# Six row groups per chunk on VectorE: three ahead of the last gate product instead of four, and two loads of u columns asked for earlier

## The chip, the cores and the metric

The kernel runs on one core of a Trainium2 chip. The metric is the device time of one execution in microseconds (us); lower is better. The engines of the core are named as the profile names them: PE (TensorE, matrix products), DVE (VectorE), ACT (ScalarE), POOL (GpSimd) and SP (SyncE, which here only starts transfers). Each has its own instruction stream, and they wait for each other by semaphores.

## The reference

One layer of a decoder trunk: window attention, RWKV-7 time mixing, a merge and a LayerNorm, and then the PEER layer, of which this case is about the last part. For every token, each of 8 heads picks 16 of 16384 single-neuron experts:

```
q = (xb @ peer_q).reshape(PEER_BLOCK, PEER_HEADS, 2, PEER_HALF)
s = jnp.einsum("bhcd,hckd->bhck", q, peer_keys)
sv, si = lax.top_k(s, PEER_TOPK)
...
gate = jax.nn.softmax(fv, axis=-1)
act = jax.nn.gelu(jnp.einsum("bhkd,bd->bhk", peer_u[eidx], xb))
return jnp.einsum("bhk,bhkd->bd", (gate * act), peer_v[eidx])
y = layer_norm(DEEPNORM_ALPHA * h + peer(h, ...), ln2_g, ln2_b)
```

The model width is 1024, all in float32. There are 1024 prompt tokens, which is 8 blocks of 128, and 8 sampled tokens.

## The kernel before, in words

The blocks' experts are computed in two ways. For the three **dense** blocks (`DENSE`) the kernel multiplies the 384 tokens with all 16384 rows of peer_u, applies Gelu, multiplies by a gate matrix G that is zero for experts that were not picked, and multiplies with all of peer_v. For the other blocks the rows of peer_u and peer_v that were picked are **fetched** one index column at a time by POOL (an indirect DMA brings 128 rows of 1024 floats, 0.52 MB), and DVE forms the dots and the weighted sums. The last three fetched blocks (`FETCHED_2`) run beside the dense blocks in the function `experts`, which is the last stage of the kernel.

`experts` walks over 16 chunks (`NCH`) of 8 tiles (`CH`) of 128 experts. In one chunk:

- PE's score stage: for each tile e, 8 matmuls over the width, from u columns (`u`) and the tokens (`hT`) into one of two PSUM buffers `sps`. The u columns lie in two pairs of tiles in SBUF, so `load_u(m)` may start when the score products of pair m-2 are done (`s_psum`). A pair is 1.05 MB.
- ACT applies Gelu to each tile of scores and writes it into `w`; DVE multiplies it by its part of G (`weigh`, the gate product).
- PE's v stage: for each of the three dense blocks k and each tile e, two matmuls of `w` with `v` into `vps`. For tile e it waits for the gate product of e (`w_done`). The v rows of a chunk (4.2 MB) are asked for when the v stage before is done, the gate matrix of a chunk (1.57 MB) when the last gate product before it is done.

All loads of u, v and G stand in SP's stream, in an order written out by hand. The row groups of the fetched blocks are woven in by hand too. One **group** on DVE (`rows.dve(dve, 8)`) is four dots, a small product of weights, four additions of rows from three groups before, and, for the first two of the three blocks, one part of the choice of experts for the next block. The fetched rows go through a ring of 10 buffers: POOL starts a fetch when DVE has used the buffer. There are 6 groups in a chunk (`PERC`), 96 in all, and three more rounds that only add. `before(e)` says how many groups stand in the slot of tile e, `behind(k)` how many stand behind the last gate product of the chunk. DVE's slot e is the gate product of tile e-2 and then the slot's group.

So in one chunk before the change DVE does: a group (slot 1), gate products 0 and 1, a group (slot 3), products 2 and 3, a group (slot 5), products 4 and 5, a group (slot 7), products 6 and 7, and two groups behind.

After the loop DVE does the last rounds of additions, the LayerNorm of the last fetched block, and those of the three dense blocks (lines 2890 to 2892).

## Time and profile before

| | us |
|---|---|
| median of 3 runs | 4342.94 (4333.28 to 4346.08) |
| the profiled execution, its time | 4383.67 |
| its span in the profile | 4381.5 |
| `experts`, from the first score product to the end of the span | 2948.75 to 4381.5 |
| PE busy in the whole span | 3782.8 (86%) |
| DVE busy in the whole span | 3027.9 (69%) |

The profiled execution takes 2.17 us more than its span, and 40.7 us more than the median of the runs. Chunks are counted from 0 to 15 here. PE's score stage of a chunk and its v stage each take about 41.4 us when nothing is waited for, 82.7 us together.

### The profile page before, as it was taken

The page shows a single profiled execution, that of the slowest core. Times are in us where ns is not written, and L with a number is a line of the kernel's source. Part 1 is how long each engine was busy: PE and PEld are TensorE (multiplying, and loading weights), DVE is VectorE, ACT ScalarE, POOL GpSimd, SP SyncE. Part 2 cuts the span into 40 slices and gives each one's busy share as a digit, 9 for nine tenths or more (in the row PEclk, how much of TensorE's full clock was granted, in tenths as well). Part 3 has the DMA queues.
Part 4 walks back from the last instruction along what each step waited for, and adds up shares of the span by engine and source line. Part 5 has one row for each costly group of instructions (what it writes and reads, how often), then busy time and mean ns, then how long its engine had stood idle before and what let it go on. Part 6 is the DMA issues. An engine that isn't in the chain of part 4 may idle for free. (4 is left out here: it accounts for less than half of the span.)

```text
span 4381.5 us, 71344 instructions
## 1 busy us (share of the span) xinstructions
PE 3782.8 (86%) x28107; PEld 2520.7 (58%) x28107; DVE 3027.9 (69%) x5964; ACT 974.3 (22%) x2046; POOL 1821.2 (42%) x1489
## 2 busy tenths in 40 slices
PE   6896888879989997888888786668999999999998
PEld 5775765546655556877765464564544454455444
DVE  0364422768988774777757378877889788977777
ACT  1351211104533332222221013770000000000001
POOL 0016100254432212333326107735666566666664
PEclk8997988889989998989989887679999999999999
DMA  7453453597766655666659633459999999999998
GB/s 191 121 163 109 154 172 146 200 359 245 264 239 235 243 206 208 225 229 227 219 209 381 247 129 50 95 155 396 403 406 391 399 412 412 382 410 413 413 403 316
DMA packets 400418, 1158.75 MB, mean 264 GB/s; under 512 B 78471, under 2 KB 157388, under 8 KB 382508
## 3 DMA queue, kind: packets, MB, share of 16 engines
q0 software_dynamic: 207216, 687.87, 43.5%
q1 hardware_dynamic: 151556, 422.07, 26.0%
q10 hardware_dynamic: 41311, 44.24, 3.0%
q8 instruction: 223, 3.65, 0.3%
q14 instruction: 112, 0.91, 0.1%
HBM read 1047.82 MB, written 116.80 MB: 266 GB/s over the span
## 5 line engine op out<-in xcount | busy, mean ns | idle before, releaser
L2814 PE MATMUL x_sps<-c_big,l_c_wo 128*128 128x384 f32 x2048 | 678.1, 493 | 33.9 <-DMA l_c_wo<-u_cols 30.2
L2822 PE MATMUL x_vps<-l_c_v,x_w 128*128 128x512 f32 x1536 | 676.9, 602 | 31.2 <-DVE x_w L2871 31.1
L387 POOL DMA_INDIRECT l_w_ring<-u_rows,k_eidx x256 | 299.6, 1170 | 922.2 <-DVE l_w_dots L443 424.3
L387 POOL DMA_INDIRECT w_ring<-u_rows,k_eidx x384 | 482.3, 1256 | 423.6 <-DVE w_dots L443 246.6
L2814 PEld LDWEIGHTS x_sps<-c_big,l_c_wo 128*128 128x128 f32 x2048 | 393.6, 193 | 318.9 <-DMA l_c_wo<-u_cols 37.4
L460 DVE SCALAR_TENSOR_TENSOR l_c_share<-w_ring,w_wts,l_c_share 128x1024 f32<-128x1024 f32 x384 | 493.4, 1285 | 76.0 <-DMA w_ring<-v_rows,k_eidx 63.0
L2822 PEld LDWEIGHTS x_vps<-l_c_v,x_w 128*128 128x128 f32 x1536 | 296.0, 193 | 406.1 <-issue 363.5
L387 POOL DMA_INDIRECT w_ring<-v_rows,k_eidx x384 | 413.1, 1076 | 143.9 <-issue 112.0
L387 POOL DMA_INDIRECT l_w_ring<-v_rows,k_eidx x256 | 300.7, 1175 | 327.0 <-DVE l_w_yacc L460 261.8
L683 PE MATMUL l_pzp<-c_big,l_c_w 128*128 128x384 f32 x960 | 327.5, 499 | 46.6 <-DMA l_c_w<-w_tiles 46.6
L460 DVE SCALAR_TENSOR_TENSOR l_w_yacc<-l_w_ring,l_w_wts,l_w_yacc 128x1024 f32<-128x1024 f32 x256 | 328.9, 1285 | 24.9 <-DMA l_w_ring<-v_rows,k_eidx 16.3
L443 DVE CUSTOM_DVE_ANT_0 w_ring<-w_ring,w_h 128x1024 f32<-128x1024 f32 x256 | 301.2, 1222 | 30.5 <-DMA w_ring<-u_rows,k_eidx 15.8
L443 DVE CUSTOM_DVE_ANT_0 l_w_ring<-l_w_ring,l_w_h 128x1024 f32<-128x1024 f32 x256 | 305.3, 1223 | 17.8 <-DMA l_w_ring<-u_rows,k_eidx 11.3
L2846 ACT ACTIVATE x_w<-x_sps 128x384 f32<-128x384 f32 x128 | 62.9, 491 | 1069.1 <-PE x_sps L2814 1001.6
L683 PEld LDWEIGHTS l_pzp<-c_big,l_c_w 128*128 128x128 f32 x960 | 185.2, 196 | 174.2 <-DMA l_c_w<-w_tiles 47.5
L1015 PE MATMUL l_qzp<-c_big,l_c_w 128*128 128x385 f32 x768 | 266.3, 502 | 14.8 <-ACT l_qz L1119 8.0
L2413 POOL DMA_INDIRECT s_G<-l_f_at_gate,l_f_at_u x128 | 208.1, 1626 | 122.3 <-DVEq L2597 68.7
L1015 PEld LDWEIGHTS l_qzp<-c_big,l_c_w 128*128 128x128 f32 x768 | 149.1, 197 | 125.0 <-issue 34.0
L2363 PE MATMUL l_f_gps<-l_f_two,l_f_one 128*128 128x128 f32 x512 | 102.8, 364 | 73.7 <-ACT l_f_two L2471 63.3
L2871 DVE TENSOR_TENSOR x_w<-x_w,l_c_wo 128x384 f32<-128x384 f32 x128 | 67.9, 559 | 132.7 <-ACT x_w L2846 123.9
L443 DVE CUSTOM_DVE_ANT_0 w_ring<-w_ring,l_c_share 128x1024 f32<-128x1024 f32 x128 | 149.6, 1220 | 5.7 <-DMA w_ring<-u_rows,k_eidx 5.2
L683 PE MATMUL e_pzp<-c_big,e_c_w 128*128 128x264 f32 x480 | 117.7, 405 | 31.9 <-DMA e_c_w<-w_tiles 20.6
(672 smaller groups left out, 6198.9 us busy)
## 6 DMA issues: line engine op xcount, KB each, us to landing
l_c_wo<-u_cols SPq DMA_DIRECT2D x64, 1024.0 KB
l_c_v<-v_rows SPq DMA_DIRECT2D x32, 2048.0 KB
e_c_w<-w_tiles SPq DMA_DIRECT2D x54, 512.0 KB, 3.6
l_c_w<-w_tiles SPq DMA_DIRECT2D x54, 512.0 KB
l_c_wo<-s_G SPq DMA_DIRECT2D x16, 1536.0 KB
s_rw<-l_q_out SPq DMA_DIRECT2D x48, 384.0 KB
s_G<-l_c_share ACTq DMA_DIRECT2D x8, 2048.0 KB
s_zT<-l_pz ACTq DMA_DIRECT2D x30, 384.0 KB
```

The source lines that it names most:

```text
L387: pool.indirect_dma_start(out=self.ring[:, r, :], out_offset=None, in_=self.A[table], in_offset=bass.IndirectOffsetOnAxis(ap=idx[:, s:s + ...
L443: V.tensor_tensor_reduce(ring[:, q % self.RING, :], ring[:, q % self.RING, :], self.h[b % self.HB][:, :], 1.0, 0.0, ALU.mult, ALU.add, sel ...
L460: self.mark(dve, V.scalar_tensor_tensor(ya[:, :], self.ring[:, q % self.RING, :], self.wts[:, s:s + 1], ya[:, :], ALU.mult, ALU.add), self ...
L683: mm = pe.matmul(zp[v % 2][:, 0:GN], w[u % 3][:, k, :], xT[:, k, x0 + g * GN:x0 + (g + 1) * GN], start=(k == 0), stop=(k == KT - 1))
L1015: mm = pe.matmul(zp[s][:, g, 0:GZ], w[q][:, k, :], xT[:, k, g * GZ:(g + 1) * GZ], start=(k == 0), stop=(k == KT - 1))
L2363: mm = pe.matmul(gps[q % 2][:, t * NKEY:(t + 1) * NKEY], one[q % 2][:, t, :], two[q % 2][:, t, :], start=True, stop=True)
L2413: pool.indirect_dma_start(out=matrix, out_offset=bass.IndirectOffsetOnAxis(ap=at_u[:, s:s + 1], axis=0), in_=gates[:, s:s + 1], in_offset= ...
L2814: mm = pe.matmul(sps[n % 2][:, 0:ND * P], u[n % 4][:, k, :], hT[:, k, :], start=(k == 0), stop=(k == KT - 1))
L2822: mm = pe.matmul(vps[k][:, x * 512:(x + 1) * 512], w[:, e, k * P:(k + 1) * P], v[:, e, x * 512:(x + 1) * 512], start=(c == 0 and e == 0), ...
L2846: act.activation(w[:, e, :], sps[n % 2][:, 0:ND * P], ACT.Gelu).then_inc(S["act_done"], 1)
L2871: V.tensor_tensor(w[:, e, :].rearrange("p (g t) -> p g t", t=TGW), w[:, e, :].rearrange("p (g t) -> p g t", t=TGW), G[:, :, e, :], ALU.mul ...
```

## The change

The number of tiles whose slots may hold a group goes from 4 to 3: the group of slot 7 is taken out from between the gate products 5 and 6, and stands behind product 7, where there are now three groups instead of two. The second edit is in SP's stream ahead of the loop: the third pair of u columns is asked for ahead of the wait for the gate matrix's stores, and the fourth right behind the load of the gate matrix, ahead of what `rows.begin` starts (the scores of the block to be chosen, the next block's h and the LayerNorm weights). Before, both pairs stood in slots 1 and 3 of chunk 0, behind all of these.

```
-        before = lambda e: 1 if e % 2 and e // 2 < PERC else 0
-        behind = lambda k: len(range(CH // 2 + k, PERC, ND))
+        AMID = CH // 2 - 1
+        before = lambda e: 1 if e % 2 and e // 2 < min(PERC, AMID) else 0
+        behind = lambda k: len(range(AMID + k, PERC, ND))
...
             rows.load_h(sp, 0)
+            load_u(2)
             for j in range(2):
                 sp.wait_ge(g_out[j], G_STORES)
             load_g(0)
+            load_u(3)
             rows.begin(sp, 1)
             for c in range(NCH):
                 for e in range(CH):
-                    if e in (1, 3):
+                    if c and e in (1, 3):
                         load_u((CH * c + e + 3) // 2)
                     rows.sp(sp, before(e))
```

SP's stream at the start of `experts` before the change. `w_h<-s_h` is the first fetched block's h, `l_c_wo<-s_G` the gate matrix, `k_scs<-s_sc` the scores for the choice, `l_c_share` the next h and the LayerNorm weights, `l_c_wo<-u_cols` a pair of u columns.

```order
L330 DMA w_h<-s_h 128x1024
L2763 DMA l_c_wo<-s_G 128x3072
L335 DMA k_scs<-s_sc 128x2048
L330 DMA l_c_share<-s_h 128x1024
L350 DMA l_c_share<-ln 128x2048
L2753 DMA l_c_wo<-u_cols 128x2048 x4
L2763 DMA l_c_wo<-s_G 128x3072
```

The same place with the change:

```order
L330 DMA w_h<-s_h 128x1024
L2754 DMA l_c_wo<-u_cols 128x2048
L2764 DMA l_c_wo<-s_G 128x3072
L2754 DMA l_c_wo<-u_cols 128x2048
L335 DMA k_scs<-s_sc 128x2048
L330 DMA l_c_share<-s_h 128x1024
L350 DMA l_c_share<-ln 128x2048
L2754 DMA l_c_wo<-u_cols 128x2048 x2
L2764 DMA l_c_wo<-s_G 128x3072
```

One pair has moved ahead of the gate matrix, one between the gate matrix and the scores; two of the four stay where they were.

DVE's stream in the last chunk before the change, from the end of the group of slot 5 to the end of the group of slot 7 and the products behind it (`x_w<-x_w,l_c_wo` is a gate product, a dot is a row with `w_ring,w_dots`, an addition one with `l_c_share<-w_ring`):

```order
L460 SCALAR_TENSOR_TENSOR l_c_share<-w_ring,w_wts,l_c_share 128x1024 x4
L2871 TENSOR_TENSOR x_w<-x_w,l_c_wo 128x384 x2
L443 ISA w_ring,w_dots<-w_ring,w_h 128x1024
L443 ISA w_dots 128x1
...
L450 TENSOR_TENSOR w_wts<-w_dots,k_gate 128x4
L460 SCALAR_TENSOR_TENSOR l_c_share<-w_ring,w_wts,l_c_share 128x1024 x4
L2871 TENSOR_TENSOR x_w<-x_w,l_c_wo 128x384 x2
```

The same place with the change:

```order
L460 SCALAR_TENSOR_TENSOR l_c_share<-w_ring,w_wts,l_c_share 128x1024 x4
L2874 TENSOR_TENSOR x_w<-x_w,l_c_wo 128x384 x4
L443 ISA w_ring,w_dots<-w_ring,w_h 128x1024
L443 ISA w_dots 128x1
...
L450 TENSOR_TENSOR w_wts<-w_dots,k_gate 128x4
L460 SCALAR_TENSOR_TENSOR l_c_share<-w_ring,w_wts,l_c_share 128x1024 x4
```

The four gate products 4 to 7 now stand together, and the group that parted them comes behind them. The streams of PE, ACT and POOL are unchanged, but for ACT's place for that group's Gelu, which is between the same instructions.

## Rows read from the trace of the kernel before

**Rows 1.** Stretches: engines' busy us, TensorE's granted clock, DMA share, GB/s.

```profile
2948.70:3049.00 100.30, 87.63 (x224) 44.94 (x225) 70.03 (x143) 6.10 (x15) 62.28 (x54) 0.91 0.99 387
3049.00:3841.20 792.20, 757.43 (x2017) 386.44 (x2016) 684.80 (x1213) 47.88 (x132) 502.36 (x430) 0.98 1.01 401
3841.20:4278.20 437.00, 422.18 (x1122) 215.87 (x1121) 324.50 (x441) 28.88 (x76) 281.10 (x243) 0.98 1.02 411
...
3980.00:4066.00 86.00, 82.19 (x219) 41.90 (x218) 62.82 (x85) 4.71 (x14) 55.44 (x48) 0.98 1.02 413
```

**Rows 2.** Waits in `experts`, by engine: total us, times, longest us.

```profile
DVE x_w L2871 <- ACT x_w L2846: 123.9, 29, 11.1
...
PE x_vps L2822 <- DVE x_w L2871: 31.1, 7, 7.9
PE x_sps L2814 <- DMA l_c_wo<-u_cols: 30.2, 9, 12.6
```

**Rows 3.** PE in order of time, chunk 8: start, us, [idle before it <-releaser].

```profile
3698.91 10.46 PE L2822 MATMUL x_vps<-l_c_v,x_w 128*128 128x512 f32 x24
3715.53 33.64 PE L2822 MATMUL x_vps<-l_c_v,x_w 128*128 128x512 f32 x72 [6.15 <-DVE x_w L2871]
```

**Rows 4.** DVE in order of time, chunk 8: the gate products around slot 7.

```profile
3701.05 1.03 DVE L2871 TENSOR_TENSOR x_w<-x_w,l_c_wo 128x384 f32<-128x384 f32 x2
...
3714.92 1.02 DVE L2871 TENSOR_TENSOR x_w<-x_w,l_c_wo 128x384 f32<-128x384 f32 x2
```

**Rows 5.** PE in order of time, chunk 0 and the score stage of chunk 1.

```profile
2948.75 22.76 PE L2814 MATMUL x_sps<-c_big,l_c_wo 128*128 128x384 f32 x64 [2.88 <-PEq L146]
2984.13 23.85 PE L2814 MATMUL x_sps<-c_big,l_c_wo 128*128 128x384 f32 x64 [12.62 <-DMA l_c_wo<-u_cols]
3007.81 41.36 PE L2822 MATMUL x_vps<-l_c_v,x_w 128*128 128x512 f32 x96
3049.01 41.44 PE L2814 MATMUL x_sps<-c_big,l_c_wo 128*128 128x384 f32 x128
```

**Rows 6.** SP's queue, chunks 0 and 1: start and us of issuing.

```profile
2961.53 0.43 SPq L335 DMA_DIRECT2D k_scs<-s_sc  x1
...
2962.95 45.39 SPq L2753 DMA_DIRECT2D l_c_wo<-u_cols  x4
...
3049.21 0.81 SPq L2758 DMA_DIRECT2D l_c_v<-v_rows  x2
3059.53 0.33 SPq L2753 DMA_DIRECT2D l_c_wo<-u_cols  x1
```

**Rows 7.** DVE, chunk 0: the first step of the choice.

```profile
2974.01 0.29 DVE L168 MAX8 k_sv<-k_scs 128x8 f32<-128x128 f32 x1 [8.13 <-DMA k_scs<-s_sc]
```

**Rows 8.** Stretches, as rows 1, in which the DMA engines moved less.

```profile
3000.00:3010.00 10.00, 10.00 (x31) 5.55 (x30) 9.75 (x15) 1.17 (x4) 7.75 (x6) 1.00 0.80 269
...
3290.00:3320.00 30.00, 30.00 (x79) 14.82 (x78) 29.23 (x39) 0.56 (x2) 17.92 (x17) 1.00 0.91 335
3730.00:3750.00 20.00, 20.00 (x49) 8.95 (x48) 19.37 (x41) 0.00 (x0) 14.91 (x12) 1.00 0.93 331
3810.00:3840.00 30.00, 30.00 (x68) 13.05 (x67) 28.36 (x39) 0.20 (x1) 23.80 (x20) 0.95 0.95 345
```

**Rows 9.** DVE at the end: last gate products, first dots of the next groups.

```profile
4325.52 1.03 DVE L2871 TENSOR_TENSOR x_w<-x_w,l_c_wo 128x384 f32<-128x384 f32 x2
4326.47 1.22 DVE L443 CUSTOM_DVE_ANT_0 w_ring<-w_ring,w_h 128x1024 f32<-128x1024 f32 x1
...
4336.52 1.22 DVE L443 CUSTOM_DVE_ANT_0 w_ring<-w_ring,w_h 128x1024 f32<-128x1024 f32 x1
```

**Rows 10.** PE, from the score stage of chunk 13 on, and chunk 15.

```profile
4122.15 23.16 PE L2814 MATMUL x_sps<-c_big,l_c_wo 128*128 128x384 f32 x64 [4.76 <-DMA l_c_wo<-u_cols]
...
4278.16 20.80 PE L2814 MATMUL x_sps<-c_big,l_c_wo 128*128 128x384 f32 x64
...
4303.95 20.80 PE L2814 MATMUL x_sps<-c_big,l_c_wo 128*128 128x384 f32 x64
```

More of the change, by code:

```diff
@@ L2743, in experts @@
         B = len(FETCHED_2)
-        before = lambda e: 1 if e % 2 and e // 2 < PERC else 0
-        behind = lambda k: len(range(CH // 2 + k, PERC, ND))
+        AMID = CH // 2 - 1
+        before = lambda e: 1 if e % 2 and e // 2 < min(PERC, AMID) else 0
+        behind = lambda k: len(range(AMID + k, PERC, ND))
         assert sum(before(e) for e in range(CH)) + sum(behind(k) for k in range(ND)) == PERC
@@ L2765, in _ @@
             rows.load_h(sp, 0)
+            load_u(2)
             for j in range(2):
@@ L2768, in _ @@
             load_g(0)
+            load_u(3)
             rows.begin(sp, 1)
@@ L2771, in _ @@
                 for e in range(CH):
-                    if e in (1, 3):
+                    if c and e in (1, 3):
                         load_u((CH * c + e + 3) // 2)
```

## The prediction, made before the changed kernel was run

> **What bounds the kernel now.** The change touches only the last stage, from 2948.75 to the end of the span at 4381.5 [rows 5], so I read that stage alone, first by stretches, then by waits, then PE and DVE in order of time. The stretches show three engines close to full at once: over chunks 1 to 14 PE is busy 1179.6 of 1229.2 us, DVE 1009.3, and the DMA share stands at 1.01 and 1.02, with 401 and 411 GB/s [rows 1]. The best stretch moved 413 GB/s, which I take as full speed [rows 1]. So the reader should see a kernel in which PE is the longest chain by a little, and in which transfers leave hardly any room: chunks 1 to 14 moved 401 x 792.2 + 411 x 437.0 = 497.3 MB, which at 413 GB/s takes 1204 us. They took 1229. The transfers' room is 25 us, and in chunk 0 another 6 us (387 x 100.3 = 38.8 MB, 94 us at full speed).
>
> The waits say what PE loses: 31.1 us in 7 waits for a gate product and 30.2 us in 9 for u columns, 12.6 of them in chunk 0 [rows 2]. One of the seven, chunk 8, shows the mechanism: PE does tiles 0 to 5 of the v stage (24 rows of 96, three quarters of the first block's third) and idles 6.15 us, until 3715.53 [rows 3]. DVE meanwhile did products 4 and 5 at 3701.05, then a group of 12.9 us, and only then products 6 and 7, at 3714.92 [rows 4]. Their scores were ready when PE's score stage ended, at 3699 [rows 3]. The group stands between.
>
> **The change part by part.**
>
> *The group of slot 7 behind the gate products.* In chunk 8 products 6 and 7 would follow at 3702, 9 us before the v stage asks for tile 6 at 3709.4, and the wait is gone. No wait of the seven is longer than 7.9 us [rows 2], less than the group that goes. What is late next: four groups now stand in a row (three behind, and slot 1 of the next chunk), and then product 0. Scores of tile e are ready about 5.2 x (e+1) us after the score stage begins (41.44 us for 8 tiles [rows 5]). Four groups of 12.9 us are 51.6, from the end of one score stage over a v stage of 41.3; product 0 comes some 11 us into the next score stage instead of 6. Tiles 0 to 3 have room, but tile 4 now stands behind only two more groups: 11 + 26 + 2 = 39 us, and PE asks for it at 41.4 + 6.9 = 48.3. So there are 9 us of room where three groups ahead of tile 6 left none (11 + 39 + 2 against 51.7). Where the choice has its heaviest parts two groups fill the 30 us from 3290 (DVE busy 29.23 of them [rows 8]), 15 us each; then it is 60 - 41 + 30 + 2 = 51, a wait of some 3 us. I keep two such waits, 6 of the 31.1 us: 25 us of PE's waits go.
>
> *The two pairs of u columns.* PE ended its first four tiles at 2971.5 and waited 12.62 us for the third pair, asked for at 2962.95 behind the gate matrix, the scores, an h and the weights [rows 5, 6]. Now it is asked for once two tiles are scored, at about 2960, and only rows are in flight: 1.05 MB beside them, there long before 2971.5. The second half then ran 23.85 us where half of a later stage is 20.7 [rows 5]; the granted clock of the stage is 0.91 [rows 1], so part of it ran at 1.2 GHz after the idle time, and those 3.1 us go too: 15.7 us. The fourth pair is asked for when four tiles are scored, at 2971.5, and is needed at 2982. The price is that this wait now stands ahead of the scores for the choice: asked for at 2961.53 and there at 2974.0 [rows 6, 7], they go out at 2972 and land behind one pair, at about 2980. DVE begins products 0 and 1 some 6 us late, but it then has one group fewer ahead of the last product. It ends its fourth group near 3012, as before, and PE starts the v stage at about 2992.5 instead of 3007.8. I cost the delay at nothing; without this cover it is 6 us.
>
> *The end.* Here the change costs. In the last chunk the score stage ends at 4324.8, products 6 and 7 come at once, at 4325.52, and from there DVE's groups follow each other without a gap [rows 9, 10]. A group without choice takes 4336.52 - 4326.47 = 10.05 us [rows 9]. With the change, products 6 and 7 still can't come ahead of the scores; DVE idles while it could have done the group, and does it behind. The end of the kernel is 10.05 us further from PE's last score stage. Nothing hides it, since these additions and three LayerNorms follow in DVE's own stream.
>
> *The sum.* PE's last score stage could begin 25 + 15.7 = 40 us earlier, if the transfers can follow. The trace of before can't show that, so I bound it. Upper end: 40 us. It exceeds the transfers' room of 31, but DVE idled 11.1 us for the last chunk's product 0 [rows 2], and with a group fewer ahead of product 7 may come another 10 us late without moving the end, so about 20 us of fetches can be put off into the last chunk. Lower end: only the stretches that ran slow behind a wait that goes are won. In the v stages that a gate wait lengthened, DVE alone draws on the transfers, more slowly than they can deliver: 30 us at 335 GB/s, 20 at 331, 30 at 345, and 10 at 269 in chunk 0 [rows 8]. Against 413 these are 5.7 + 4.0 + 4.9 + 3.5 = 18 us. I take the middle, 29 us, because both ends rest on stretches of this stage and neither is nearer. 29 - 10 = 19 us off the profiled execution's 4383.67, to 4365. The runs' median is 40.7 us below that execution; I take the same 19 us off it: 4324 us.
>
> **A rule that speaks against it.** A v load is asked for at 3049.21 and a pair of u columns behind it at 3059.53, and PE used that pair at 3069.7 with no wait [rows 5, 6]. So SP's queue brought 5.24 MB in 20.5 us, 256 GB/s or 62% of the whole, beside a row ring that had work throughout. The Trainium skill (DMA: Bandwidth & Descriptors, Queues, rings and completion order) says that each DMA engine goes round the queues that have work, a packet from each, and takes a queue's descriptors in order. If that meant halves, the 5.24 MB would take 25.4 us at 206 GB/s, and PE would wait 4.7 us in every chunk. The trace disagrees for most chunks, so the sum leaves it out.
>
> **The rivals.**
>
> *The transfers swallow it.* PE runs ahead and meets u columns and starved groups instead; the last score stage begins 0 to 18 us earlier, and the end lies between 8 us earlier and 10 later: 4335 to 4353, middle 4343. For it speaks a DMA share of 1.01, against it that the slow stretches lie just behind the waits that go. That the change does not do what it says (its waits come back at other tiles) ends here as well. Chance 0.25.
>
> *Slower by u waits.* With PE ahead the ring never fills, SP's queue gets a smaller share in the score stages, and u columns come late as in chunk 13: 4.76 us and 23.16 - 20.7 = 2.4 us at the lower clock [rows 10], 7.2 us a chunk. From six more such chunks on, 43 us, the kernel is slower by over 13 us; in all 14, 101 - 40 + 10 = 71 us slower, 4414. The 62% above speak against it. Chance 0.07.
>
> *Slower by DVE.* If DVE never idles, a chunk takes 6 groups and 4.5 us of gate products. Its busy time less 63 us of products is 946 us for 84 groups, 11.3 each, 12.2 with its waits for rows: 78 us, well under PE's 82.7. Against the present 87.8 us a chunk it decides from a group of 13.9 us on; at 14.2 it would be 6 x 0.3 x 14 = 25 us slower at the last score stage, 4378 with the end. Chance 0.05.
>
> **How the numbers follow.** A measurement of this kernel tells a change from none at about 0.3%, which is 13 us: under 4330 is faster, above 4356 slower. The forecast has chance 0.63 and its own range 4313 to 4335; some 0.11 of it lies above 4330. Faster 0.52, same 0.11 + 0.25 = 0.36, slower 0.12. The range reaches from 4304, a little beyond the case in which all of PE's 40 us come through, to 4350, which takes in nearly all of the first rival.
>
> **What would show it.** PE waits for gate products under 10 us in total, and none in chunks 8 and 9 over 3. No wait for the third pair, a v stage of chunk 0 from about 2993, DVE's first choice step near 2980. The last score stage at about 4249 instead of 4278. DVE idle before the last chunk's product 7, and from there to its last instruction 10 us more than before. Slow stretches in the v stages of chunks 3, 8 and 9 gone. I am wrong if u waits beyond chunk 0 grow past 35 us, or if the last score stage begins after 4260.

## The result, and the profile after

The changed kernel takes 4354.60 us (median of 15 runs, 4341.94 to 4366.03) beside 4344.34 (15 runs of the kernel before on the same chip, 4330.77 to 4361.09). The ratio is 1.0028, with a 95% interval of 1.0017 to 1.0039: about 12 us slower, within the 0.3% that the prediction called no change, and on the other side of it than the forecast.

The profiled execution of the changed kernel took 4342.70 us (span 4340.5), 41 us less than that of the kernel before. This is no contradiction: `experts` began at 2906.22 instead of 2948.75, so 42.5 us of the difference lie in stages that the change does not touch, and come from one execution to the next. From here on I compare lengths inside `experts`, not times since the start, and use several profiles of each kernel.

Here are the stretches of the changed kernel, with columns as in [rows 1]: chunk 0, chunks 1 to 14, the last chunk to the end of the span, and then three of its slow stretches.

```profile
2906.20:2993.60 87.40, 84.98 (x224) 43.67 (x225) 55.18 (x113) 6.33 (x15) 49.64 (x43) 0.97 0.99 381
2993.60:4226.60 1233.00, 1177.06 (x3138) 600.84 (x3137) 1018.62 (x1679) 78.20 (x208) 772.18 (x677) 0.98 1.01 404
4226.60:4340.50 113.90, 87.75 (x237) 44.61 (x235) 87.79 (x110) 14.63 (x35) 53.90 (x50) 0.90 0.83 316
...
3250.00:3260.00 10.00, 10.00 (x27) 4.94 (x26) 9.82 (x14) 0.00 (x0) 6.78 (x6) 1.00 0.71 228
...
3690.00:3700.00 10.00, 10.00 (x27) 4.78 (x26) 9.69 (x19) 0.00 (x0) 5.72 (x6) 1.00 0.91 320
...
3750.00:3790.00 40.00, 35.85 (x80) 15.95 (x81) 39.09 (x55) 0.41 (x2) 25.71 (x22) 0.91 0.91 324
```

For the kernel before, [rows 1] cuts chunks 1 to 14 differently and leaves out the last chunk, so this is the same view of it in the same cuts:

```profile
3049.00:4278.20 1229.20, 1179.62 (x3138) 602.30 (x3137) 1009.29 (x1654) 76.76 (x208) 783.46 (x673) 0.98 1.01 404
4278.20:4381.50 103.30, 87.75 (x237) 44.61 (x235) 81.77 (x103) 14.74 (x35) 49.64 (x42) 0.94 0.81 310
```

Three things stand in these rows. Chunk 0 is 13 us shorter (87.40 instead of 100.30). The last chunk is 10.6 us longer (113.90 instead of 103.30). And the fourteen chunks between, where 25 us of waits were to go, take 1233.0 instead of 1229.2 us, at the same 404 GB/s. Multiplied out, the bytes say the same: before, 38.8 + 496.6 + 32.0 = 567.4 MB in the three parts; after, 33.3 + 498.1 + 36.0 = 567.4 MB. The shorter chunk 0 moved 5.5 MB less, which then had to be moved later: 1.5 MB of it in chunks 1 to 14, 4.0 MB in the last chunk.

The 404 GB/s are a mean of two parts. Here are chunks 1 to 10 and chunks 11 to 14, first of the kernel before, then of the changed one:

```profile
3049.00:3924.20 875.20, 840.21 (x2242) 428.93 (x2241) 749.04 (x1302) 55.36 (x149) 555.66 (x477) 0.98 1.01 402
3924.20:4278.20 354.00, 339.41 (x898) 173.38 (x897) 260.25 (x353) 21.40 (x59) 227.80 (x196) 0.97 1.02 410
```

```profile
2993.60:3874.20 880.60, 841.15 (x2241) 428.98 (x2240) 751.61 (x1319) 56.45 (x149) 554.86 (x481) 0.98 1.01 401
3874.20:4226.60 352.40, 335.91 (x898) 171.87 (x897) 267.01 (x361) 21.74 (x59) 217.32 (x197) 0.98 1.02 413
```

The last four of them run at 413 GB/s with the change, for 352 us; the first ten stay at 401. The slow stretches above lie among these ten, in the v stages of chunks 3, 8 and 9, and those are the three chunks in which [rows 8] has them before. In all of them DVE is busy nearly throughout (9.82 of 10 us, 9.69 of 10, 39.09 of 40). So 413 can be held with all loads, and what the changed kernel did not do is hold it in chunks 1 to 10.

The waits of the changed kernel inside `experts`, with columns as in [rows 2] and DVE's waits for fetched rows added:

```profile
DVE l_c_share L460 <- DMA w_ring<-v_rows,k_eidx: 141.7, 76, 4.9
DVE w_ring L443 <- DMA w_ring<-u_rows,k_eidx: 60.9, 28, 9.6
PE x_vps L2825 <- DVE x_w L2874: 44.4, 10, 8.8
DVE x_w L2874 <- ACT x_w L2849: 14.3, 5, 4.5
PE x_sps L2817 <- DMA l_c_wo<-u_cols: 14.0, 10, 7.4
```

PE's gate waits did not go from 31.1 to 6 us, they went to 44.4 in 10 waits. What did go are DVE's waits for scores, 123.9 us before and 14.3 now. In their place DVE waits 203 us for fetched rows; before it was 84 (63.0 and 21.0). DVE has hardly any slack in front of PE any more, and what it waits for is rows.

Chunk 9 shows how this looks. First PE, as in [rows 3], then DVE, as in [rows 4]:

```profile
3697.06 41.44 PE L2817 MATMUL x_sps<-c_big,l_c_wo 128*128 128x384 f32 x128
3738.34 7.03 PE L2825 MATMUL x_vps<-l_c_v,x_w 128*128 128x512 f32 x16
3754.15 36.08 PE L2825 MATMUL x_vps<-l_c_v,x_w 128*128 128x512 f32 x80 [8.78 <-DVE x_w L2874]
```

```profile
3708.47 1.28 DVE L460 SCALAR_TENSOR_TENSOR l_c_share<-w_ring,w_wts,l_c_share 128x1024 f32<-128x1024 f32 x1 [0.80 <-DMA w_ring<-v_rows,k_eidx]
...
3713.42 1.28 DVE L460 SCALAR_TENSOR_TENSOR l_c_share<-w_ring,w_wts,l_c_share 128x1024 f32<-128x1024 f32 x1 [3.67 <-DMA w_ring<-v_rows,k_eidx]
3716.01 1.28 DVE L460 SCALAR_TENSOR_TENSOR l_c_share<-w_ring,w_wts,l_c_share 128x1024 f32<-128x1024 f32 x1 [1.30 <-DMA w_ring<-v_rows,k_eidx]
...
3722.24 1.03 DVE L2874 TENSOR_TENSOR x_w<-x_w,l_c_wo 128x384 f32<-128x384 f32 x2
...
3753.54 1.96 DVE L2874 TENSOR_TENSOR x_w<-x_w,l_c_wo 128x384 f32<-128x384 f32 x4
```

Product 0 comes 25 us into the score stage (3722.24 less 3697.06), not 11. The four additions of the group ahead of it wait for their rows one by one. Products 4 to 7 follow two groups later, at 3753.54, and PE, which had finished 16 of 96 rows of its v stage, idles 8.78 us. All ten gate waits of the changed kernel stand there, ahead of the last 80 matmuls of a v stage: the wait is now for tile 4. In the 10 us from 3690, just ahead of this score stage, transfers ran at 320 GB/s, and 20 us later DVE waited for them.

In chunk 0 the second edit did what it said. PE's start of the stage, as in [rows 5]:

```profile
2906.22 43.72 PE L2817 MATMUL x_sps<-c_big,l_c_wo 128*128 128x384 f32 x128 [2.88 <-PEq L146]
2949.78 7.03 PE L2825 MATMUL x_vps<-l_c_v,x_w 128*128 128x512 f32 x16
2959.21 34.60 PE L2825 MATMUL x_vps<-l_c_v,x_w 128*128 128x512 f32 x80 [2.40 <-DVE x_w L2874]
```

PE's 128 score matmuls run without a break, and the v stage begins 43.6 us into the stage instead of 59.1. The first choice step on DVE, as in [rows 7], stood 25.3 us into the stage and now stands 35.6 us into it:

```profile
2941.84 0.29 DVE L168 MAX8 k_sv<-k_scs 128x8 f32<-128x128 f32 x1 [21.13 <-DMA k_scs<-s_sc]
```

At the end, as in [rows 9], the last gate product and the first dot behind it:

```profile
4268.63 1.49 DVE L2874 TENSOR_TENSOR x_w<-x_w,l_c_wo 128x384 f32<-128x384 f32 x3
4273.71 0.56 DVE L2874 TENSOR_TENSOR x_w<-x_w,l_c_wo 128x384 f32<-128x384 f32 x1 [3.59 <-ACT x_w L2849]
4274.19 1.22 DVE L443 CUSTOM_DVE_ANT_0 w_ring<-w_ring,w_h 128x1024 f32<-128x1024 f32 x1
...
4284.24 1.22 DVE L443 CUSTOM_DVE_ANT_0 w_ring<-w_ring,w_h 128x1024 f32<-128x1024 f32 x1
```

DVE idles for the last score and then has one group of 10.05 us more to do than before; it is busy 87.79 us in this part instead of 81.77.

### The profile page after: what moved, and what is told of

Its sections match the earlier page's. It is cut to its first block and busy times, and to the rows that moved or that the text cites. A ratio compares the mean times of both kernels' runs of the same rounds, so it can differ in the third digit from the quotient of the medians.

```text
span 4340.5 us, 71344 instructions
## 1 busy us (share of the span) xinstructions
PE 3751.0 (86%) x28107; PEld 2506.1 (58%) x28107; DVE 3029.2 (70%) x5964; ACT 975.3 (22%) x2046; POOL 1794.3 (41%) x1489
## 3 DMA queue, kind: packets, MB, share of 16 engines
q0 software_dynamic: 207216, 687.87, 43.9%
## 5 line engine op out<-in xcount | busy, mean ns | idle before, releaser
L2825 PE MATMUL x_vps<-l_c_v,x_w 128*128 128x512 f32 x1536 | 679.3, 603 | 44.4 <-DVE x_w L2874 44.4
L387 POOL DMA_INDIRECT w_ring<-u_rows,k_eidx x384 | 462.6, 1205 | 409.1 <-DVE w_dots L443 201.1
L2817 PEld LDWEIGHTS x_sps<-c_big,l_c_wo 128*128 128x128 f32 x2048 | 390.3, 191 | 297.6 <-DMA l_c_wo<-u_cols 20.9
L683 PE MATMUL l_pzp<-c_big,l_c_w 128*128 128x384 f32 x960 | 325.0, 496 | 47.2 <-DMA l_c_w<-w_tiles 47.2
L2413 POOL DMA_INDIRECT s_G<-l_f_at_gate,l_f_at_u x128 | 205.9, 1608 | 123.1 <-DVEq L2597 68.0
L2363 PE MATMUL l_f_gps<-l_f_two,l_f_one 128*128 128x128 f32 x512 | 103.5, 365 | 73.0 <-ACT l_f_two L2471 66.5
L2363 PEld LDWEIGHTS l_f_gps<-l_f_two,l_f_one 128*128 128x128 f32 x512 | 89.3, 262 | 85.7 <-ACT l_f_two L2471 73.2
```

The source lines that it names most:

```text
L387: pool.indirect_dma_start(out=self.ring[:, r, :], out_offset=None, in_=self.A[table], in_offset=bass.IndirectOffsetOnAxis(ap=idx[:, s:s + ...
L683: mm = pe.matmul(zp[v % 2][:, 0:GN], w[u % 3][:, k, :], xT[:, k, x0 + g * GN:x0 + (g + 1) * GN], start=(k == 0), stop=(k == KT - 1))
L2363: mm = pe.matmul(gps[q % 2][:, t * NKEY:(t + 1) * NKEY], one[q % 2][:, t, :], two[q % 2][:, t, :], start=True, stop=True)
L2413: pool.indirect_dma_start(out=matrix, out_offset=bass.IndirectOffsetOnAxis(ap=at_u[:, s:s + 1], axis=0), in_=gates[:, s:s + 1], in_offset= ...
L2817: mm = pe.matmul(sps[n % 2][:, 0:ND * P], u[n % 4][:, k, :], hT[:, k, :], start=(k == 0), stop=(k == KT - 1))
L2825: mm = pe.matmul(vps[k][:, x * 512:(x + 1) * 512], w[:, e, k * P:(k + 1) * P], v[:, e, x * 512:(x + 1) * 512], start=(c == 0 and e == 0), ...
```

## The experiments

**Theory 1**, the first rival of the prediction: transfers bind chunks 1 to 14, and what PE gains at one tile it loses at another. **Theory 2**: the late scores of the block to be chosen put DVE behind from chunk 0 on, and it never recovers. **Theory 3**: DVE's own work, not its rows, binds it. Two later theories, **A** and **B**, are given where they come up.

All runs together, in us. "Stage" is `experts` from the first score product to the end of the span of one profiled execution; chunk 0, 1 to 14 and the last are its parts; "gate" is PE's waits at the tile boundaries of the v stages, where it waits for a gate product (the profile names no releaser for some of them and calls them "issue": 11.2 us in e7_before_again, 2.7 in e8_after_again, 10.8 in e12_split_v, 1.6 in e5_before_no_v, 21.2 in e11_before_copy_v; they are counted); the ratio is that of run times to the kernel before on the same chip, with its interval.

| run | stage | chunk 0 | 1 to 14 | last | gate | ratio |
|---|---|---|---|---|---|---|
| before | 1432.8 | 100.3 | 1229.1 | 103.3 | 31.1 | |
| e7_before_again | 1429.6 | 97.3 | 1229.0 | 103.4 | 26.3 | |
| after | 1434.3 | 87.4 | 1232.9 | 113.9 | 44.4 | 1.0028 (1.0017 to 1.0039) |
| e8_after_again | 1452.6 | 86.9 | 1252.9 | 112.7 | 37.4 | |
| e15_after_third | 1437.4 | 87.6 | 1236.9 | 112.9 | 47.2 | |
| e1_rows | 1442.6 | 97.0 | 1232.9 | 112.7 | 43.9 | 1.0029 (1.0016 to 1.0041) |
| e2_u | 1432.4 | 100.0 | 1228.9 | 103.5 | 49.6 | 1.0016 (1.0003 to 1.0030) |
| e3_u_scores | 1426.2 | 94.3 | 1225.8 | 106.1 | 39.2 | 0.9995 (0.9980 to 1.0010) |
| e4_last | 1435.7 | 86.8 | 1235.9 | 113.0 | 49.1 | 1.0006 (0.9992 to 1.0019) |
| e14_last_again | 1429.0 | 87.7 | 1226.2 | 115.1 | 35.4 | |
| e12_split_v | 1429.2 | 94.4 | 1231.4 | 103.5 | 43.5 | 0.9980 (0.9967 to 0.9993) |
| e5_before_no_v | 1370.1 | 97.0 | 1169.7 | 103.4 | 10.0 | 0.9861 (0.9816 to 0.9907) |
| e6_after_no_v | 1358.4 | 86.6 | 1159.0 | 112.7 | 2.3 | 0.9858 (0.9794 to 0.9922) |
| e13_last_no_v | 1345.3 | 87.2 | 1154.7 | 103.4 | 2.6 | 0.9841 (0.9780 to 0.9902) |
| e9_copy_at_s | 1488.3 | 87.4 | 1288.1 | 112.7 | 58.9 | 1.0141 (1.0114 to 1.0168) |
| e10_copy_at_v | 1496.8 | 87.5 | 1286.2 | 123.1 | 69.6 | 1.0129 (1.0099 to 1.0158) |
| e11_before_copy_v | 1495.7 | 97.1 | 1288.2 | 110.4 | 96.3 | 1.0131 (1.0101 to 1.0161) |

### The same kernels again

Runs e7_before_again, e8_after_again and e15_after_third have no edit. They tell how far one profile can be trusted.

> The kernel before once more, for a second profile of it: how far experts' stage (1433 us) and its waits (31 us for gate products, 18 for u columns behind chunk 0) differ between two executions. Expected within 5 us for the stage, with up to 40 us of difference ahead of it.

> The changed kernel once more. Expected: experts' stage 1434 to 1446 us, last chunk 113 to 114, gate waits 35 to 50 us, most of them at tile 4. If the median's 10 us lie in the stage, it is nearer to 1443 than to 1434.

> The changed kernel for a third profile (stage 1434.3 and 1452.6 before). Expected: chunk 0 at 87 us, chunks 1 to 14 at 1233 to 1253, last chunk 112.7 to 114, so a stage 5 to 15 us above the 1431 of the kernel before.

The second profile of the kernel before has the same 1229.0 us in chunks 1 to 14. Its waits view names 15.1 us of gate waits, where the first had 31.1, but two more stand at the same place (behind 24 matmuls of a v stage) without a releaser. Here is the longer one, of chunk 3, on PE, and DVE's products 6 and 7 that end it:

```profile
3265.69 33.73 PE L2822 MATMUL x_vps<-l_c_v,x_w 128*128 128x512 f32 x72 [7.74 <-issue]
```

```profile
3265.08 1.02 DVE L2871 TENSOR_TENSOR x_w<-x_w,l_c_wo 128x384 f32<-128x384 f32 x2
```

With both (7.74 and 3.50 us, in chunks 3 and 6) the gate waits are 26.3 us in 6 waits beside 31.1 in 7: the waits that the change goes for do repeat. The 4.8 us fewer did not make the fourteen chunks shorter; waits for u columns in them are 24.2 us beside 17.6. The changed kernel took 1232.9, 1252.9 and 1236.9 us there, with gate waits of 44.4, 37.4 and 47.2. The 1252.9 is an outlier that I cannot place; its transfers ran at 399 GB/s, and PE idled 70 us in it, beside 56 in the first profile. Chunk 0 (86.9 to 87.6) and the last chunk (112.7 to 113.9) repeat well. The means over profiles, 2 and 3 of them, give chunk 0 -11.5, chunks 1 to 14 +11.9, the last +9.8: together 10 us slower, near the 12 that the runs show.

### One half of the change at a time

**e1_rows**: the kernel before with DVE's new order, and SP's stream as it was.

```diff
-        before = lambda e: 1 if e % 2 and e // 2 < PERC else 0
-        behind = lambda k: len(range(CH // 2 + k, PERC, ND))
+        AMID = CH // 2 - 1
+        before = lambda e: 1 if e % 2 and e // 2 < min(PERC, AMID) else 0
+        behind = lambda k: len(range(AMID + k, PERC, ND))
```

> Only the row groups are moved; SP's stream is that of before. Theory 1 (the transfers bound chunks 1 to 14, so what PE wins at product 6 is lost to starved groups, and the end costs 10 us): experts' stage 1440 to 1446 us against 1433 in the profile of before, ratio 1.002 to 1.003; the last chunk 113 to 114 us from its score stage to the end of the span. Theory 2 (the scores that come 10 us later behind the fourth pair leave DVE behind for good, and this is what brings the gate waits back): without that edit the gate waits fall under 20 us and the last score stage begins over 10 us earlier than before, ratio 0.998 to 1.000.

Gate waits of 43.9 us without the late scores (the first choice step came 22.1 us into the stage): Theory 2 falls. DVE's new order by itself keeps chunk 0 at 97.0, adds 3.8 us to chunks 1 to 14 and 9.3 to the last, 13 us against e7_before_again (10 against the first profile); the runs show 13 (ratio 1.0029). The changed kernel has the same ratio, 1.0028, although its chunk 0 is 10 us shorter (87.4 beside 97.0): what the second edit gains in chunk 0 is not seen in the whole.

**e2_u**: the changed kernel with DVE's old order, so only SP's stream differs from before.

```diff
-        AMID = CH // 2 - 1
+        AMID = CH // 2
```

> Only the two pairs of u columns are asked for earlier; DVE's order is that of before. Theory 1: chunk 0 is 12 to 15 us shorter, chunks 1 to 14 give nearly all of it back, last chunk 103 us as before: ratio 0.998 to 1.001. Theory 2: DVE starts 10 us late and stays behind, more gate waits than before (over 40 us): ratio 1.001 to 1.003.

Chunk 0 gained nothing, 100.0 us. PE has no wait for u columns there but two for gate products. PE in chunk 0:

```profile
2957.56 7.03 PE L2825 MATMUL x_vps<-l_c_v,x_w 128*128 128x512 f32 x16
2966.87 3.70 PE L2825 MATMUL x_vps<-l_c_v,x_w 128*128 128x512 f32 x8 [2.28 <-DVE x_w L2874]
2980.51 34.04 PE L2825 MATMUL x_vps<-l_c_v,x_w 128*128 128x512 f32 x72 [9.94 <-DVE x_w L2874]
```

With four groups ahead of product 7 there is no cover for scores that come 10 us later: DVE waits 20.6 us for them, its groups slip, and PE waits for tile 6 (24 rows done, as in [rows 3]) 9.94 us. The u wait of 12.6 us turned into this one. The numbers are those that were expected by Theory 2 (49.6 us of gate waits, ratio 1.0016), and chunk 0 is not the 12 to 15 us shorter of Theory 1. But DVE doesn't stay behind: 12.2 of the gate waits lie in chunk 0, product 0 comes 6 to 11 us into the score stage from chunk 1 on, as before, and chunks 1 to 14 take 1228.9 us. So the late scores cost time in chunk 0 alone.

**e3_u_scores**: e2_u, with the scores asked for ahead of the fourth pair.

```diff
             load_g(0)
-            load_u(3)
             rows.begin(sp, 1)
+            load_u(3)
```

> Only the u columns earlier, DVE's order as before, but what brings the scores for the choice stands ahead of the fourth pair. DVE's first choice step should come 26 to 28 us after the first score product instead of 36. Theory 1: the time is that of the run with both pairs ahead, within 0.1%. Theory 2: 0.2 to 0.3% faster than that run, ratio 0.996 to 0.998 to the kernel before.

DVE had the scores at 30.6 us into the stage, still later than the 26 to 28 that I expected:

```profile
2960.03 0.29 DVE L168 MAX8 k_sv<-k_scs 128x8 f32<-128x128 f32 x1 [16.10 <-DMA k_scs<-s_sc]
```

The 9.94 us wait is gone, a u wait of 7.62 stays, and chunk 0 takes 94.3. The profile has the shortest stage of all kernels with their full loads, 1426.2 us, but the runs cannot tell it from before. Against e2_u it is 6 us faster (medians 4345.77 and 4351.97 on the same chip), 0.14%, about the 5.7 us by which chunk 0 is shorter. That is more than the 0.1% of Theory 1 and less than the 0.2 to 0.3% of Theory 2.

**e4_last** and **e14_last_again** (the same kernel twice): the changed kernel, with the old order of DVE in the last chunk alone. `before` and `behind` take the chunk as an argument everywhere.

```diff
-        AMID = CH // 2 - 1
-        before = lambda e: 1 if e % 2 and e // 2 < min(PERC, AMID) else 0
-        behind = lambda k: len(range(AMID + k, PERC, ND))
+        AMID = lambda c: CH // 2 if c == NCH - 1 else CH // 2 - 1
+        before = lambda c, e: 1 if e % 2 and e // 2 < min(PERC, AMID(c)) else 0
+        behind = lambda c, k: len(range(AMID(c) + k, PERC, ND))
```

> The changed kernel, but with four groups ahead of the last gate product in chunk 15 alone. Both theories: the last chunk falls from 114 to 103 or 104 us, so 10 us (0.23%) less than the changed kernel. Theory 1: with that the kernel is level with before, ratio 0.998 to 1.001. If it stays at 1.002 or more, the cost is not at the end.

> The same order in chunk 15 with all loads, for a second profile: its first had a last chunk of 113.0 us, although its ratio was 1.0006. If DVE is late at the last score stage (groups of slots 3 and 5 begin over 2 us later than 11.5 and 22.5 into it), the last chunk stays near 113; if it is in time, 103 to 105.

The runs improve on those of the changed kernel (1.0006 beside 1.0028, intervals that just overlap), but the profiles don't show it where it was expected: the last chunk takes 113.0 and 115.1 us, not 103. (The profiled execution of e4_last is the slowest of its 12 runs, 4377.53 us where their median is 4351.83.) DVE in the last chunk of e14_last_again, whose score stage begins at 4238.18:

```profile
4251.69 1.28 DVE L460 SCALAR_TENSOR_TENSOR l_c_share<-w_ring,w_wts,l_c_share 128x1024 f32<-128x1024 f32 x1 [4.88 <-DMA w_ring<-v_rows,k_eidx]
...
4257.97 1.03 DVE L2873 TENSOR_TENSOR x_w<-x_w,l_c_wo 128x384 f32<-128x384 f32 x2
...
4294.29 1.03 DVE L2873 TENSOR_TENSOR x_w<-x_w,l_c_wo 128x384 f32<-128x384 f32 x2
```

The last two products come at 56.1 us into the stage (4294.29), where before they came at 47.4 [rows 9, 10]. The groups of slots 3 and 5 begin 20.9 and 34.8 us into it, not 11.5 and 22.5, so the case of a late DVE in the expectation is the one that came. DVE reached the last chunk waiting for rows, and in these two profiles the rows and not the place of the group decide when the last product can be done. Whether this holds for the other runs is not shown: their ratio of 1.0006 is what the order's 10 us would give.

### Fewer bytes, and the same bytes elsewhere

**e5_before_no_v** and **e6_after_no_v**: the kernels before and after without the v loads of chunks 1 to 15 (63 MB of 567), so that PE multiplies with chunk 0's rows of peer_v.

```diff
                     rows.sp(sp, behind(k))
-                if c + 1 < NCH:
-                    load_v(c + 1)
...
                         pe.wait_ge(S["w_done"], CH * c + e + 1)
-                        if c and e % QUAD == 0:
-                            pe.wait_ge(v_in[e // QUAD], 16 * c)
```

> The kernel before, but chunks 1 to 15 load no rows of peer_v and use those of chunk 0, so 4.2 of 35 MB a chunk are not moved; that part of the result is left out. Theory 1: with 12% fewer bytes the transfers no longer bind; u waits vanish and gate waits fall under 15 us, since groups are no longer starved in the score stage; chunks 1 to 14 take 83 to 84 us each. Theory 3 (DVE's own work binds, whatever the transfers): gate waits stay near 31 us, chunks near 86.

> The changed kernel with the same part left out. Theory 1: gate waits under 10 us, chunks 1 to 14 at 83 us each, so the last score stage begins as early as in the run before or up to 15 us earlier, and the end costs its 10 us: ratio of this run to the run before 0.999 to 1.002. Theory 3: gate waits stay over 30 us, at tile 4.

Chunks 1 to 14 of e5_before_no_v:

```profile
3043.90:4213.60 1169.70, 1159.10 (x3137) 596.56 (x3136) 1009.53 (x1654) 76.41 (x208) 767.98 (x672) 1.00 0.97 373
```

and of e6_after_no_v:

```profile
3023.00:4182.00 1159.00, 1155.29 (x3137) 595.71 (x3136) 1022.78 (x1685) 77.30 (x208) 777.26 (x678) 1.00 0.98 380
```

In e6_after_no_v PE is busy 1155.3 of 1159.0 us at the full granted clock, and its gate waits in the whole stage are 2.3 us. DVE did the same work as in the changed kernel, 1022.8 us of it, and was in time: Theory 3 falls. With 12% fewer bytes in a chunk the change does between these two kernels what the prediction said in kind: 10.4 us off chunk 0, 10.7 off chunks 1 to 14 with 10.0 us of gate waits to win, and 9.3 more in the last chunk. Of the 10.7, 9.7 are chunk 9 (92.2 to 82.5 us), where e5_before_no_v still waits 6.38 us for tile 6 at 353 GB/s: that wait is DVE's order and the choice in its groups, not transfers, and with all loads the change turns it into one of 8.78 us for tile 4. These are single profiles. The runs, with intervals of half a per cent, are too coarse to show the 12 us that this leaves.

**e13_last_no_v**: e6_after_no_v with e4_last's order of the last chunk.

> The changed kernel with four groups ahead of the last gate product in chunk 15 alone, and without the v loads of chunks 1 to 15 (their rows are replaced by those of chunk 0). With those bytes gone DVE is not late when the last score stage begins. If the end costs 10 us because the third group stands behind the last gate product, the last chunk falls from 112.7 (changed kernel without v loads) to 103 or 104 us here. If it stays over 110, the end of the changed kernel is longer for another reason.

Here the forecast's term for the end stands by itself. DVE at the end:

```profile
4207.01 1.03 DVE L2869 TENSOR_TENSOR x_w<-x_w,l_c_wo 128x384 f32<-128x384 f32 x2
4207.95 1.22 DVE L443 CUSTOM_DVE_ANT_0 w_ring<-w_ring,w_h 128x1024 f32<-128x1024 f32 x1
```

The last products come 47.4 us into the last chunk (its score stage began at 4159.64), exactly as in [rows 9, 10], and the chunk takes 103.4. The 9.3 us beside e6_after_no_v's 112.7 are the price of the group's place; nothing else differs between the two kernels.

**Theory A**: the bytes of a chunk bind, wherever in the chunk they are moved. **Theory B**: the v load at the start of a score stage starves the group of slot 1 there, and elsewhere in the chunk it would not. **e9_copy_at_s** moves the same v bytes as the changed kernel at the same place, but into device memory, so that PE doesn't wait for them. **e10_copy_at_v** moves them half a chunk earlier, beside the v stage ahead. **e11_before_copy_v** does this to the kernel before. In all three PE again multiplies with chunk 0's rows.

```diff
             def load_v(c):
-                sp.wait_ge(S["v_psum"], ND * c)
                 for a in range(CH // QUAD):
-                    sp.dma_start(v[:, QUAD * a:QUAD * (a + 1), :], A["v_quads"][CH // QUAD * c + a]).then_inc(v_in[a], 16)
+                    sp.wait_ge(v_in[a], 16 * (c - 1))
+                    sp.dma_start(A["spare"][a], A["v_quads"][CH // QUAD * c + a]).then_inc(v_in[a], 16)
...
                         load_u(CH // 2 * (c + 1) + m)
+                    load_v(c + 1)
                     load_g(c + 1)
...
-                if c + 1 < NCH:
-                    load_v(c + 1)
```

(In e9_copy_at_s the first wait and the place of the call stay as they were.)

> The changed kernel in which chunks 1 to 15 use the peer_v rows of chunk 0 (their own are left out of the result), but the same 4.2 MB are still read, at the same place (start of the score stage), into a spare array in device memory. It shows whether the copy stands for the load. Both theories: chunks 1 to 14 near 1230 us again (1159 without the bytes), gate waits over 30 us at tile 4, product 0 over 12 us into the score stage in most chunks.

> As the run with the copy at the score stage, but the 4.2 MB are asked for at the start of the v stage ahead, where the slow stretches lie. Theory A (the bytes of a chunk bind, wherever they stand): chunks 1 to 14 within 10 us of that run. Theory B (the v load at the start of the score stage starves just the group of slot 1 that the change leaves there): at least 35 us fewer for chunks 1 to 14, gate waits under 15 us.

> The kernel before with the copy at the start of the v stage (same part of the result left out). Theory A: chunks 1 to 14 within 10 us of the two copy runs of the changed kernel. Theory B: it gains less from the place than the changed kernel, since it has one group fewer in the shadow of the load: 10 to 30 us more than the changed kernel with the copy there.

Chunks 1 to 14 of e9_copy_at_s:

```profile
3040.00:4328.20 1288.20, 1191.88 (x3138) 606.36 (x3137) 1024.46 (x1685) 78.64 (x208) 768.92 (x679) 0.96 1.00 388
```

of e10_copy_at_v:

```profile
3034.90:4321.10 1286.20, 1182.17 (x3138) 604.86 (x3137) 1018.95 (x1680) 78.10 (x208) 761.00 (x676) 0.96 1.00 387
```

and of e11_before_copy_v:

```profile
3032.50:4320.70 1288.20, 1179.01 (x3137) 603.70 (x3136) 1008.02 (x1660) 76.80 (x208) 765.18 (x669) 0.96 0.99 383
```

I expected chunks 1 to 14 of e9_copy_at_s near 1230 us and missed by 58: with the copy in place of the load a chunk takes 4.1 us more, at 388 GB/s and a DMA share of 1.00. What the three say together still holds, because they share this cost. With the transfers made heavier, the fourteen chunks take 1288, 1286 and 1288 us, whichever order DVE has and wherever the copy stands. PE idles 96, 104 and 109 us in them, and only the kind of its waits differs: in the whole stage 58.9 us for gates and 33.2 for u columns in e9_copy_at_s, 69.6 and 1.5 in e10_copy_at_v, which also waits in its score stages for a PSUM buffer that ACT has not yet read (12.0 us named, most of 30.6 without a releaser), 96.3 for gates in e11_before_copy_v, and no u wait there behind chunk 0. This is what Theory A expected, from one profile of each; the runs agree (medians 4445, 4440 and 4441 us). Theory B in its strong form, that the place of the v load costs time by itself, is not borne out: with the copy beside the v stage product 0 still comes 13 to 35 us into the score stage.

**e12_split_v**: e3_u_scores, with the second half of the v rows asked for behind the u pair of slot 1 instead of at the start of the score stage.

```diff
                         load_u((CH * c + e + 3) // 2)
+                        if e == 1:
+                            load_v(c, 1)
...
-                    load_v(c + 1)
+                    load_v(c + 1, 0)
```

> A whole kernel again: DVE's order of before, u columns earlier with the scores ahead of the fourth pair, and the second half of each v load asked for behind the first u pair of the chunk instead of with the first half. Theory A: no change against that kernel without the split, ratio to before 0.998 to 1.001. Theory B: first groups less starved, u waits behind chunk 0 under 8 us (12.8), 5 to 10 us faster: 0.997 to 0.998.

It is the only kernel with all its loads that the runs show to be faster than the one before: ratio 0.9980 (12 runs beside 17), 9 us. Its profile does not say by what. Chunks 1 to 14 take 1231.4, with 9.5 us of u waits where Theory B had asked for under 8 (e3_u_scores has 12.8), and 0.9980 lies on the border of both expectations, so it does not decide between them; the gain that can be placed is chunk 0's, 94.4 beside 97.3 and 100.3. Against e3_u_scores (0.9995) the intervals overlap. The most that any order tried here gained is 0.2%, and the change under study loses 0.3%.

## Why the prediction was wrong

*What bounds the kernel now.* The reading was right that transfers had hardly any room (25 us in chunks 1 to 14), and 413 GB/s was a fair full speed to take: the changed kernel holds it over 352 us. What was wrong is that PE, freed of its waits, would take this room. The mean of these fourteen chunks is 404 GB/s in both profiles of the kernel before (404, 405) and no higher in those of the changed one (404, 399, 402). Chunks 1 to 10 run at 402 GB/s before and at 401 after, and the room still lies there. The Trainium skill (Perfetto Trace Analysis, Roofline) bounds a core that is active alone at about 435 GB/s, all of its 16 DMA engines together. No slice of any profile here is above 415, so by this case's rows the room was smaller than the page would make it.

*The gate waits, 31.1 to 6 us: wrong.* The group of slot 7 did move out of the way, and no wait for tile 6 is left. What is late next was named rightly (tile 4, with 9 us of room) but priced wrongly. I put product 0 at 11 us into the score stage with groups of 12.9 us. It came at 12 to 29 us in most chunks. Before, the group of slot 1 began 3 to 16 us ahead of the score stage, took 10 to 15 us, and never waited for a row. With the change it begins between 5 us ahead of the score stage and 8 us behind its start, beside the v load, and takes 10 to 24 us, up to 12 of them waits for rows. An estimate from rows of this case: a group uses 8 fetched rows of 0.52 MB, and with the 4.2 MB of the v load these are 8.4 MB, 20 us at 413 GB/s; in the chunks in which product 0 came later than 20 us the group took 19 to 24. That the v load beside it is the whole reason is not shown, since e10_copy_at_v moves it away and the group is still late. The check against the old order was also off: "11 + 39 + 2 against 51.7" puts product 0 at 11 us, where it stood at 6 to 9 in all chunks but one before, so the waits for tile 6 came with longer groups: in chunk 8 product 6 stood 57.3 us into the score stage, 49 behind product 0, with three groups between. I read the two DVE rows together: idle time for scores fell from 123.9 to 14.3 us, and waits for rows rose from 84 to 203, as if the idle time had been what let the ring fill. That is a reading of the sums, no experiment isolates it. With 12% fewer bytes the estimate holds: in e6_after_no_v product 0 stands at 6 to 17 us, and 2.3 us of waits are left.

*Chunk 0, 15.7 us: right in mechanism, 13 us in size* (100.3 to 87.4; against e7_before_again 10). The third pair's wait is gone, the v stage begins 43.6 us into the stage (predicted 43.8), and a gate wait of 2.4 us is new. The delay of the scores was predicted as 6 us and was 10. They were asked for when I said, 23.5 us into the stage instead of 12.8, but I gave them 8 us to land where [rows 6, 7] show 12.5, and they took 12.1. Under DVE's new order the delay cost 2.4 us, nearly the nothing that I claimed, and under the old one 12 us (e2_u), more than the 6 that I gave for it without cover. That the 13 us of chunk 0 don't show in the whole (e1_rows) is another matter.

*The end, +10.05 us: right.* The last chunk takes 9.3 to 10.6 us more, and e13_last_no_v beside e6_after_no_v shows that it is the group's place. With all loads the old order in the last chunk alone did not shorten it in two profiles, in which rows hold the last products (e4_last, e14_last_again).

*The sum: this is the step that failed.* The term is PE's gain at its last score stage, taken as 29 us between 18 and 40. The last score stage began 1320.3 us after the first instead of 1329.4, 9 us earlier, and 1339.9 and 1324.5 in the other two profiles: 1328.2 in the mean, beside 1327.9 for the two profiles of the kernel before. The gain was nothing. "Lower end: only the stretches that ran slow behind a wait that goes are won", 18 us, was no lower end. Slow stretches are not tied to the waits behind which I found them. I expected those in the v stages of chunks 3, 8 and 9 to be gone, and the changed kernel has one in each of the three (228 GB/s from 3250, 320 from 3690, 324 from 3750), though the waits for tile 6 are gone. What they keep in common, before and after, is a DVE that is busy nearly throughout, and the change takes no work from DVE. That DVE's work on the choice makes them, since it frees no buffer of the row ring meanwhile, is a reading of these rows; no run leaves the choice out. The upper end supposed that PE's 40 us are there to be had, but the change removes no bytes, and the gate waits that go at tile 6 come back at tile 4 (44.4 us). The lower end should have been zero, and that was the first rival, with its 4335 to 4353: "its waits come back at other tiles". The median lies 2 us beyond it. Of the 5.5 MB that a shorter chunk 0 puts off, 1.5 MB are 3.7 us at 404 GB/s, about the 3.8 by which chunks 1 to 14 are longer in this profile; the other 4.0 fall into the last chunk, where transfers run at 316 GB/s and do not bind.

*The rule on queues.* I left it out of the sum, since SP's queue had 62% of the whole. With the change, the slower case of it, *slower by u waits*, did not come either: u waits behind chunk 0 are 14.0 us in 10 waits, before they were 17.6. The 4.7 us in every chunk that halves would give (DMA: Bandwidth & Descriptors, Queues, rings and completion order, in the Trainium skill) are not seen in this trace: nine of the ten u waits are of 1.2 us or less, the tenth of 7.4.

*Slower by DVE.* DVE was late, but not by its own work: 1018.6 us busy in 1233.0. The rival's price of 12.2 us for a group was too low in the chunks where rows starve, and it decided nothing, as e6_after_no_v shows.

What stays open: how much of the 12 us lies in chunks 1 to 14. The profiles give 1229 and 1229 before, 1233, 1237 and 1253 after, and e14_last_again and e4_last, whose order there is that of the changed kernel, 1226 and 1236. What makes the slow stretches of chunks 3, 8 and 9 was not isolated, and the size of the ring of fetched rows was never varied. And why e4_last's runs are better than those of the changed kernel by 0.2%, which none of its profiles shows.

## What to carry to other kernels

When PE, DVE and the DMA engines are all near full, divide the bytes of the stage by the best rate that it holds over several chunks (413 GB/s here, 98% of the length of chunks 1 to 14) before believing any wait on PE. If that is within 1 or 2% of the stage's length, a wait that is removed is likely to come back elsewhere, and the lower end of the forecast is no gain. A cheap test is a kernel with some of the loads left out: if the edit gains there and not in the real one, the bytes are part of the bound. An engine that consumes prefetched rows and idles less may wait for the rows instead; an edit that removes its idle time has to be charged for that. And a second profile of the unchanged kernel costs little. Read its waits by their place and not only by the releaser that the profile names: 11.2 of 26.3 us of gate waits were called "issue" in one, and a sum by name would have taken them for gone.

## What was not expected of the hardware

- Stages ahead of `experts`, the same in all these kernels, end up to 46 us apart from one profiled execution to another (2906.2 to 2952.6, on several chips), 36 us for the changed kernel alone, while chunks 1 to 14 of the kernel before repeat to 0.2 us.
- Chunks 1 to 14 went from 1233 to 1288 us for 58.7 MB copied within device memory instead of loaded into SBUF (388 instead of 404 GB/s).
- The scores, 1.05 MB, take 12.5 us from issue to landing before [rows 6, 7], and 12.1 with the change (asked for at 2929.71, used at 2941.84), where 1.05 MB alone are 2.5 us at 413 GB/s. In e3_u_scores, asked for right behind the third pair and the gate matrix, they take 17.3. SP's row with the change:

```profile
2929.71 0.43 SPq L335 DMA_DIRECT2D k_scs<-s_sc  x1
```

What the scores share with in that time was not tested.
